# Convolution norm: the two sums over the partitions in four column tiles, the quarters added by a product inside the next unit

## The reference, cut to what matters

```python
a = a_in[..., :D_CONV] * jax.nn.sigmoid(a_in[..., D_CONV:])
a = causal_depthwise_conv(a, conv_a_w) + conv_a_b        # 31 taps
a = jax.nn.silu(layer_norm(a, ln_a_g, ln_a_b))
y_a = a @ w_a_out + b_a_out
...
def layer_norm(x, g, b):
    mu = jnp.mean(xf, axis=-1, keepdims=True)
    var = jnp.mean(jnp.square(xf - mu), axis=-1, keepdims=True)
    y = (xf - mu) * lax.rsqrt(var + LN_EPS)
    return (y * g + b)
...
m = sigmoid(g_a) * y_a + sigmoid(g_b) * y_b + sigmoid(g_c) * y_c
return m @ w_mix_out
```

## Time and profile before

| | us |
|---|---|
| median of three runs | 2087.11 (2086.47 to 2088.25) |
| profiled execution, its own time | 2087.27 |
| its span, first to last instruction | 2085.5 |
| PE busy | 2016.8 (97%) |
| DVE busy | 1126.5 (54%) |
| ACT busy | 708.1 (34%) |

### The profile page before, as it was taken

One profiled execution on the slowest core, in us unless ns is written; L12 is line 12 of the kernel. 1 busy time (PEld: TensorE's weight loads), 2 busy tenths in 40 slices (PEclk: granted clock), 3 DMA queues, 4 the chain that ended last, 5 costly groups with the idle time before them and its releaser, 6 DMA issues.

```text
span 2085.5 us, 28522 instructions
## 1 busy us (share of the span) xinstructions
PE 2016.8 (97%) x11524; PEld 1335.6 (64%) x11524; DVE 1126.5 (54%) x1733; ACT 708.1 (34%) x934; POOL 3.0 (0%) x10
## 2 busy tenths in 40 slices
PE   7999999999999999999999999999999999999998
PEld 7999998853333333333333333388788898888887
DVE  6998898652222222221222222268798676657764
ACT  4434554421111111111111111175645443545543
POOL 0000000000000000000000000000000000000000
PEclk9999999999999999999999999999999999999999
DMA  9545759999999999999999999973488755646752
GB/s 339 192 167 178 283 195 370 361 407 415 428 427 428 425 429 429 428 428 428 429 429 429 428 429 429 417 241 107 153 288 277 262 195 209 212 162 204 250 173 80
DMA packets 188011, 654.91 MB, mean 314 GB/s; under 512 B 10992, under 2 KB 76528, under 8 KB 162704
## 3 DMA queue, kind: packets, MB, share of 16 engines
q1 hardware_dynamic: 187920, 653.59, 80.5%
HBM read 652.50 MB, written 1.06 MB: 313 GB/s over the span
## 4 chain that ended last, share of the span: by engine, by line
PE 73%; DMA 22%; DVE 3%; ACT 1%; issue 0%; SPq 0%; ACTq 0%; DVEq 0%
DMA ring<-w_down 21%; PE front L1028 19%; PE front L1079 15%; PE front L1350 10%; PE pair L1378 7%; PE front L1049 5%; PE pair L1049 3%; PE front L1051 2%; PE front L986 2%; PE pair L1418 1%; PE pair L1051 1%; PE pair L1330 1%; PE front L1360 1%; DMA arena<-w_gu 1%; DMA ring<-w_in 1%; DVE ring_low L2356 1%
## 5 line engine op out<-in xcount | busy, mean ns | idle before, releaser
L2356 DVE TENSOR_TENSOR ring_low<-ring,w_high 128x2048 fp32r<-128x2048 f32 (+1 forms) x179 | 404.7, 2267 | 133.7 <-ACT w_high L1731 133.2
L1350 PE MATMUL front<-ring,arena 128*64 128x512 f32 x1808 | 403.1, 595 | 9.7 <-DMA ring<-w_gu 9.6
L1731 ACT ACTIVATE w_high<-ring 128x2048 fp32r<-128x2048 f32 (+1 forms) x179 | 338.1, 1893 | 178.7 <-PE front L1079 78.4
L1028 PE MATMUL front<-x_parts,w_high 128*128 128x256 f32 x2048 | 373.1, 285 | 11.3 <-DVE ring_low L2556 9.1
L2888 DVE TENSOR_TENSOR arena<-front,par 128x512 f32<-128x512 f32 x64 | 44.0, 688 | 621.9 <-PE front L1360 621.9
L1028 PEld LDWEIGHTS front<-x_parts,w_high 128*128 128x128 f32 x2048 | 320.7, 192 | 15.2 <-issue 11.7
L1350 PEld LDWEIGHTS front<-ring,arena 128*64 128x64 f32 x1808 | 125.8, 137 | 277.7 <-issue 244.2
L1028 PE MATMUL front<-x_parts,ring_low 128*128 128x256 f32 x1024 | 290.2, 283 | 0.0
L1079 PE MATMUL front<-w_high,arena_r 128*128 128x512 f32 x736 | 229.3, 390 | 1.3 <-DVE ring_low L2356 0.7
L1378 PE MATMUL pair<-ring,arena 128*64 128x512 f32 x864 | 195.3, 597 | 27.6 <-DMA ring<-w_down 27.6
L1028 PEld LDWEIGHTS front<-x_parts,ring_low 128*128 128x128 f32 x1024 | 197.0, 192 | 0.0
(11 more groups left out here) (391 smaller groups left out, 2351.4 us busy)
## 6 DMA issues: line engine op xcount, KB each, us to landing
ring<-w_gu SPq DMA_DIRECT2D x113, 2048.0 KB, 23.6
ring<-w_down SPq DMA_DIRECT2D x57, 2048.0 KB, 25.4
ring<-ffn_w_gate_up SPq DMA_DIRECT2D x44, 1024.0 KB, 7.9
ring<-ada_w SPq DMA_DIRECT2D x20, 2048.0 KB, 8.4
ring<-ret_w_in SPq DMA_DIRECT2D x12, 2048.0 KB, 7.9
ring<-w_in SPq DMA_DIRECT2D x10, 2048.0 KB, 8.0
arena<-w_gu SPq DMA_DIRECT2D x10, 2048.0 KB, 14.6
ring<-ffn_w_down SPq DMA_DIRECT2D x8, 2048.0 KB, 8.7
```

The costliest lines, as they stand in the source:

```text
L1028: mm = pe.matmul(acc_bank[:, ch * T:(ch + 1) * T], w[:, k, ch * P:(ch + 1) * P], xs[:, kk, :], start=kk + ch + n == 0, stop=kk == b.kc - 1 ...
L1350: mm = pe.matmul(bank[b][64 * o:64 * o + 64, :], xgT[:, k // 4, k % 4, :], gu_cols(b_in, j, D * o + 512 * b), start=k == 0, stop=k == DC - 1)
L1731: nc.scalar.activation(high_part(u), raw_part(u), ACT.Copy).then_inc(sem("w_high"), 1)
L2356: V.tensor_tensor(low_part(u), raw_part(u), high_part(u).bitcast(F32), ALU.subtract).then_inc(sem("w_low"), 1)
```

## The change

The two sums are split into column tiles. `norm_parts` puts chunk c's product into rows 32 * (c % 4) to + 32 of the bank, so that four products with 32 columns of ones stand side by side, each tile adding two chunks. Every one of the 32 rows of a quarter holds the same partial sum. ACT copies this [128, 256] result into `rstd` (`norm_parts_in`), and `norm_whole` multiplies it by the full matrix of ones, which adds the quarters (32 times over) and spreads them to all partitions, into the other half of the same bank; the scale becomes 1/(32 D). This product is called inside the next unit of `xk[1]`, after four chunks of its first half. On ACT the high part of unit 1 of `xv[0]` now comes behind the second copy. On DVE `early_sum(2)` between the low part of `xv[0]` and the low part of the convolution is gone, and the later `early_sum(8)` is `early_sum(10)`.

```diff
+                            if between and ch == 0 and k == 4:
+                                between()
...
-            def norm_mean(n):
+            def norm_parts(q, src, name, squared=None):
+
                 for c in range(DC):
-                    mm = pe.matmul(bank[4][:, 0:T], n.mean[:, :], n.src[:, c, :], start=c == 0, stop=c == DC - 1)
-                mm.then_inc(sem("ln_mean"), 1)
...
+                    if squared and c % (DC // 2) == 0:
+                        pe.wait_ge(sem("ln_sq"), squared + c // (DC // 2))
+                    o = 32 * (c % 4)
+                    mm = pe.matmul(bank[q][o:o + 32, 0:T], ones[:, 0:32], src[:, c, :], start=c < 4, stop=c >= 4,
+                                   skip_group_check=True)
+                mm.then_inc(sem(name), 1)
+
+            def norm_whole(q, name):
+
+                pe.wait_ge(sem("ln_row"), q - 3)
+                pe.matmul(bank[q][:, T:2 * T], ones[:, :], rstd[:, :], start=True, stop=True).then_inc(sem(name), 1)
...
-            norm_mean(n_conv)
-            feature(xk[1], s_mem, units=(0,))
-            norm_var(n_conv)
-            feature(xk[1], s_mem, units=(1,))
+            norm_parts(4, conv, "ln_mean")
+            feature(xk[1], s_mem, units=(0,), between=lambda: norm_whole(4, "ln_mean"))
+            norm_parts(5, sq, "ln_var", 1)
+            feature(xk[1], s_mem, units=(1,), between=lambda: norm_whole(5, "ln_var"))
...
+            def norm_parts_in(q, name):
+
+                act.wait_ge(sem(name), 1)
+                nc.scalar.activation(rstd[:, :], bank[q][:, 0:T], ACT.Copy).then_inc(sem("ln_row"), 1)
+
+            norm_parts_in(4, "ln_mean")
             norm_square(n_conv)
+            high_until(units_of(xv[0])[0])
+            norm_parts_in(5, "ln_var")
             high_until(units_of(xv[0])[1])
             norm_std(n_conv)
...
             low_until(units_of(xk[1])[1] + 2)
-            early_sum(2)
             split_low("conv")
             low_until(units_of(branch_out["a", 0])[1])
-            early_sum(8)
+            early_sum(10)
             mix_in("a", 2, 0, 0)
```

More of the change, by code:

```diff
@@ L1008, in first_units, with feature @@
                 products(acc_v, low_part(v), x[0], range(b.kc), stop=True).then_inc(sem("mm_done"), 1)
-            def feature(b, x, units=(0, 1, 2, 3, 4, 5), turned=None):
+            def feature(b, x, units=(0, 1, 2, 3, 4, 5), turned=None, between=None):
                 if turned:
@@ L1864, in norm_std @@
             def norm_std(n):
-                act.wait_ge(sem("ln_var"), n.n)
+                act.wait_ge(sem("ln_var"), 2 * n.n)
                 if n.n > 1:
                     act.wait_ge(sem("ln_out"), 2 * (n.n - 1))
-                nc.scalar.activation(rstd[:, :], bank[5][:, 0:T], ACT.Sqrt, scale=1.0 / D, bias=n.eps).then_inc(sem("ln_std"), 1)
+                nc.scalar.activation(rstd[:, :], bank[5][:, T:2 * T], ACT.Sqrt, scale=1.0 / (32 * D), bias=n.eps).then_inc(sem("ln_row"), 1)
             def ada_take(s):
@@ L2369, in norm_centre @@
             def norm_centre(n):
-                dve.wait_ge(sem("ln_mean"), n.c)
-                V.scalar_tensor_tensor(out=n.src, in0=bcast(bank[4][:, 0:T], DC), scalar=-1.0 / D, in1=n.src, op0=ALU.mult,
+                dve.wait_ge(sem("ln_mean"), 2 * n.c)
+                V.scalar_tensor_tensor(out=n.src, in0=bcast(bank[4][:, T:2 * T], DC), scalar=-1.0 / (32 * D), in1=n.src, op0=ALU.mult,
                                    op1=ALU.add).then_inc(sem("ln_cen"), 1)
@@ L2375, in norm_finish @@
             def norm_finish(n, affine=True):
-                dve.wait_ge(sem("ln_std"), n.n)
+                dve.wait_ge(sem("ln_row"), 3 * n.n)
                 link(V.reciprocal(rstd[:, :], rstd[:, :]))
```

## The result

| | before | changed |
|---|---|---|
| median of four runs, us | 2086.79 (2085.89 to 2088.25) | 2102.39 (2098.66 to 2106.19) |
| profiled execution, us | 2087.27 | 2098.66 |
| its span, us | 2085.5 | 2096.9 |
| PE busy | 2016.8 | 2015.5 |

The changed kernel takes 1.0074 times as long (95% interval 1.0062 to 1.0086). It is slower, as forecast, but by 15.6 us in the median, where 9.4 were forecast and the range ended at 2098.8. The four runs were 2098.66, 2099.12, 2105.66 and 2106.19. One execution of the kernel before, in a later session, took 2890.21 us at a granted clock of 0.655; it is counted in that session's median but in no ratio.

What follows compares the result with a forecast made beforehand. TensorE bounded the kernel around the norm, with a1 only 0.8 us of slack behind a transfer. Later a1 (+8.2 us) plus slow restart (1.2) gave +9.4: 2096.7 for the profiled execution, 2096.5 against the median, range 2094.0 to 2098.8.

Steps and rivals of the forecast that it cites:

- The saving on TensorE: TensorE at the norm's two sums: each tiled sum 1.19 us instead of 3.45, norm_whole 0.43; saved 3.66 us.
- The new waits: Around the norm: ACT's copy takes 0.47 us, TensorE doesn't wait for it, DVE centres 0.4 us earlier.
- Where the saving ends: At a0's start: TensorE waits for a0's low part until 301.7, leaving 1.5 of 3.66 us.
- SP's release: Moved early-sum steps end at 305.4, so SP issues tile 4 and a1 9.4 us later than 295.97.
- Rivals (2): At the norm's sums: column tiles don't run side by side, each sum still 3.45 us; +11.7, 2098.8; chance 0.04.
- (4): At SP's issue: the moved steps don't hold SP, a1 lands as before; gain 1.2 us, 2085.9; chance 0.05.
- (5): At a0: as (4), and no wait for a0 either, all 3.66 us come through; 2083.4; chance 0.03.
- The landing: Before a1: tile 4 lands 7.8 us after issue, a1's weights 12.8; a1 starts at 322.9, +8.2 us.
- The restart: TensorE at a1, after its standstill: first passes at 1.2 GHz, adding 1.2 us; bounds 0 and 1.7.
- rival (1): At a1: no slow restart, the same path without 1.2 us; 2095.3; chance 0.25.
- Does it reach the end: From the mix blocks through the experts' stage: the shift passes on, moving the total by 8.2 to 9.4 us.
- Rival (3): Transfers between 340 and 440 us: their slack takes up about half the shift; 2092; chance 0.05.

Runs made afterwards that it cites:

- experiment 6: Changed kernel with early-sum steps moved forward, plus a0's first high part before the silu and its low part before the convolution's: median 2083.98 us, ratio 0.9982.
- experiment 1: Changed kernel with the two early-sum steps put back between the low parts of xv[0] and the convolution: median 2088.64 us, ratio 1.0008.
- the changed kernel's second trace: The changed kernel run again with nothing altered, to see its spread: median 2098.97 us over six runs, ratio 1.0060; the traced execution took 2099.92.
- experiment 2: Kernel before, with only the two early-sum steps moved behind a0's low parts: median 2099.20 us, ratio 1.0059.
- experiment 4: Changed kernel with 48 unused ones products between a0 and a1 to keep TensorE busy: median 2099.26 us, ratio 1.0053.
- experiment 8: Changed kernel with unused ones products in both TensorE standstills, 10 ahead of a0 and 50 between a0 and a1: median 2098.76 us, ratio 1.0046.
- experiment 5: Changed kernel with the two early-sum steps moved forward, ahead of the norm's end, instead of back: median 2087.47 us, ratio 1.0003.
- experiment 7: Kernel before, with its old sums, given the same ACT and DVE reordering as experiment 6: median 2087.37 us, ratio 0.9998.

## Why the prediction was right or wrong

**The saving on TensorE: right.** 3.66 us were forecast for both sums together, and in experiment 6 `xv[0]` begins 3.7 us earlier. A tiled sum is recorded with 1.00 us, and the 12 passes behind the first one with 1.62 where 1.44 is undisturbed: 1.18 together, the 1.19 taken. `norm_whole` is 0.45 (0.43). The Trainium skill ("TensorEngine Tiling (Array Packing)", Key Properties) states that tiles work independently of each other and that different ones can run products at the same time. The 1.00 us agree, since one after another the products would take 3.45.

**The new waits: right.** ACT's copy took 0.38 us, and DVE began to centre at 277.29 for the 276.97 forecast. In this trace all of the program is late from its start on: its first product begins at 9.42 instead of the 9.13 of the earlier trace rows. Less these 0.29 us the centring is at 277.00, 0.4 us earlier than before, as worked out.

**Where the saving ends, and SP's release: right.** a0 waits for its low part, forecast for 301.7, measured at 301.81 (experiment 1) and 301.85 (the changed kernel's second trace). SP issues tile 4 at 305.66 and 305.38 in the changed kernel's first two traces, for 305.4. Experiment 2 shows that the two moved steps are the whole loss, and experiment 1 that putting them back takes it away. Rivals (2), (4) and (5) fall with the first rows.

**The landing: mis-sized.** The term took 7.8 us for tile 4 from one row, with +0.5 as upper bound. Seven traces with the late issue give 8.3 to 9.6, and a1's transfer 13.3 to 14.6 in place of 12.8. The core moved 386 to 390 GB/s meanwhile, as before, so it isn't a slower memory. The first of the mix tiles behind landed 18.8 us after its own issue in the changed kernel and 19.0 in experiment 1, where tile 4 took 7.7: at the same throughput the bytes fell to the queued tiles in other shares. Why, is not settled. That is some 1.1 us of the miss in the traced execution.

**The restart: right in kind, mis-sized.** Forecast 1.2, bounds 0 to 1.7. Measured, as a1's passes less 11.52: 1.64, 1.69, 1.93, 2.31 and 2.83 us. The forecast's only row was the program's start, and the upper bound was set just above it, with no second row behind it; three of five traces pass it. The slow restart came in all five, so rival (1) falls, and experiments 4 and 8 show that it goes away when TensorE is kept busy. The rule of the Trainium skill ("TensorE: Matmul & The Clock Gate", Part 1), that an idle array falls back to 1.2 GHz, agrees with the granted clock of 0.50 from 318 to 327 us.

**Does it reach the end: right.** In the traced execution it was 11.4 us at the mix blocks and 11.4 at the end. Rival (3) falls: no slack took any of it up. For the traced execution the terms add: 9.4 + 0.29 at the start + 1.16 landing + 0.44 restart + 0.1 for small differences = 11.4, and 2087.27 + 11.4 is its 2098.66.

**The range: wrong.** It ended at 2098.8. The steps that failed are the two terms above, the landing (7.8 taken, 8.3 to 9.6 measured) and the restart (1.2 taken, 1.6 to 2.8 measured). Each had bounds from one row of one execution, and so the usual executions stand at 2097 to 2100, already on the range's edge. And the four measured runs held two of 2105.66 and 2106.19, which puts their median at 2102.39: for the spread from one execution to the next the range had no term. With all twelve executions the median would be 2099.2, still outside. What makes the long ones is open; their lower mean clock (0.995) is all that was measured of them. A late landing of `arena<-w_gu` and a granted clock of 0.66 behind it cost 3.4 and 4.3 us in the longest executions of experiments 4 and 8; that may be a part of it, but it was not seen in the changed kernel itself. Long executions are not its own alone: experiment 1 had four of twelve above 2092, experiment 5 two of ten, and before itself one of 2095.17 in 17. That the prediction named the direction and nearly the size of the usual execution is earned; that its profiled execution (2098.66) falls inside the range is in part luck, since it was among the shorter ones.

**Not thought of:** that the short standstill ahead of a0, which the prediction has only as 1.5 us of 3.66 that are left, can cost the clock too. It cost 1.7 us in the traces of experiments 4 and 5.

## What to carry to other kernels

A step that lets go of a buffer is also the release of a transfer, and of all that stands behind it in a queue that issues in order, as SP's program does here: before such cheap work is moved behind something else, find who waits for its last piece. Two steps of 0.76 us each, moved by 9.7 us, cost 11.5 us, three times what the real improvement gave. A saving on the engine that bounds reaches the end only if the next work on it has its inputs earlier as well; here that took two moved calls on ACT and DVE, which alone were worth nothing.

## What the runs showed of the hardware

- The granted clock can fall after a standstill of TensorE of only 1.95 us: to 0.50, some 1.3 us into the work that followed, in two traces (a0 13.23 for 11.52; a0 and a1 24.76 for 23.03). In five others (experiment 1 and the four traces of the changed kernel), with a standstill of about the same length, it stayed at 1.00 there. It makes equal programs differ by 1.7 us.
- After 9.9 to 11.2 us of standstill the passes came at 0.21 us each for about 3 to 5.5 us, which cost 1.6 to 2.8 us (five traces). The cost doesn't follow the standstill's length: 9.94 us cost 2.31, 10.62 cost 1.64.
- At equal throughput (386 to 390 GB/s) the first of several queued 2 MB tiles landed 7.8 and 7.7 us after its issue in the kernel before and in experiment 1, after 8.3 to 9.6 in the seven traces with the late issue, and after 8.4 to 8.6 in the three with the early one (experiments 5 to 7).
- From 4 to 14 us the profile gives a granted clock of 1.00 while passes of 256 columns come 0.21 us apart from 9.13 to 12.05; in mid-program the same 0.21 us stand beside a granted clock of 0.50. So the printed clock isn't to be relied on at the start.
